# Transposes between the blocks of a sum, and a mixing norm whose first projections take unscaled rows

## What is computed

```
x = x + 0.5 * ffn(rms_norm(x, g_ffn1))
h = rms_norm(x, g_mix);  parts = split(h @ w_in)      # xr, gr, qb, ckv, qi, ki, wi, qc, kc, vc, f, ga, gb, gc
o_a = rglru(conv(xr)) * gelu(gr);  o_b = top-k latent attention(qb, ckv, qi, ki, wi);  o_c = forgetting attention(qc, kc, vc, f)
x = x + (sigmoid(ga)*(o_a@w0) + sigmoid(gb)*(o_b@w1) + sigmoid(gc)*(o_c@w2)) @ w_out
x = x + memory_cross_attention(rms_norm(x, g_xattn), rms_norm(mem, g_mem))
x = x + 0.5 * ffn(rms_norm(x, g_ffn2))
rms_norm(x, g) = x * rsqrt(mean(x*x) + 1e-6) * g;     ffn(h) = (silu(h@w_g) * (h@w_u)) @ w_down
```

## Time and profile before

| | |
|---|---|
| Median of 3 runs | 1418.57 us |
| The profiled execution: its time, its span | 1418.43 us, 1416.6 us |
| Mean granted TensorE clock | 0.997 |
| Busy: TensorE, VectorE, ScalarE, POOL | 1379.8, 945.6, 777.5, 132.3 us |
| HBM read | 241.18 MB |

### The profile page before, as it was taken

The page is one execution under the profiler, slowest core; times in us unless marked ns, Lnnn a source line. Parts: engine busy times, 40 slices in busy tenths (PEclk is TensorE's granted clock), DMA queues, the critical chain, the costliest instruction groups (busy, mean ns, idle before and its releaser), DMA issues.

```text
span 1416.6 us, 23830 instructions
## 1 busy us (share of the span) xinstructions
PE 1379.8 (97%) x8846; PEld 1228.3 (87%) x8846; DVE 945.6 (67%) x1456; ACT 777.5 (55%) x1378; POOL 132.3 (9%) x219
## 2 busy tenths in 40 slices
PE   6999999999999999999999999999999999999998
PEld 5888879988999888888888888898989989888886
DVE  5666666878666567666676666658777556666665
ACT  5554554745654466555564555566556445655544
POOL 4010000021420100000010000000224001100000
PEclk9999999999999999999999999999999999999999
DMA  8677664544545555666656667546454554466662
GB/s 239 187 205 208 196 179 149 163 138 148 170 132 175 183 144 165 191 180 199 184 174 185 198 185 205 149 136 201 134 160 138 166 191 144 129 203 179 198 187 74
DMA packets 286385, 243.38 MB, mean 172 GB/s; under 512 B 14345, under 2 KB 263609, under 8 KB 286305
## 3 DMA queue, kind: packets, MB, share of 16 engines
q1 hardware_dynamic: 284176, 236.77, 55.4%
q10 hardware_dynamic: 1600, 4.25, 0.9%
q0 software_dynamic: 528, 1.26, 0.5%
HBM read 241.18 MB, written 1.27 MB: 171 GB/s over the span
## 4 chain that ended last, share of the span: by engine, by line
issue 64%; PE 25%; DVE 3%; ACT 3%; POOL 2%; DVEq 1%; POOLq 1%; DMA 1%; ACTq 0%
PE work L1548 15%; PE work L1623 2%; PE work L1570 2%; PE acc L1585 1%; PE work L1627 1%; ACT w_hi L507 1%; POOL diag L721 1%; PE acc L1775 1%; DVE w_lo L515 1%; POOLq L720 1%; PE work L1763 1%; DVE score L1350 1%; ACT lg L1033 1%; DVEq L1238 0%; PE work L1698 0%
## 5 line engine op out<-in xcount | busy, mean ns | idle before, releaser
L515 DVE TENSOR_TENSOR w_lo<-raw,w_hi 128x1024 fp32r<-128x1024 f32 x444 | 550.5, 1260 | 105.8 <-ACT w_hi L507 104.2
L507 ACT ACTIVATE w_hi<-raw 128x1024 fp32r<-128x1024 f32 (+1 forms) x442 | 450.7, 1053 | 25.6 <-PE acc L1585 25.6
L1623 PE MATMUL work<-act,w_hi 128*128 128x512 f32 x1408 | 443.6, 396 | 9.5 <-DVE w_lo L515 5.5
L1548 PE MATMUL work<-act,w_hi 128*128 128x256 f32 x1696 | 317.8, 286 | 3.2 <-DVE act L1131 1.7
L1627 PEld LDWEIGHTS work<-act,w_lo 128*128 128x128 f32 x1408 | 265.0, 188 | 62.6
L1627 PE MATMUL work<-act,w_lo 128*128 128x256 f32 x1408 | 277.6, 279 | 0.0
L1548 PEld LDWEIGHTS work<-act,w_hi 128*128 128x128 f32 x1696 | 267.4, 191 | 10.4 <-issue 5.8
L1548 PE MATMUL work<-act,w_lo 128*128 128x256 f32 x848 | 239.8, 283 | 0.0
L1623 PEld LDWEIGHTS work<-act,w_hi 128*128 128x128 f32 x1408 | 217.8, 189 | 13.4 <-issue 10.4
L821 ACT ACTIVATE gu_s<-work 128x256 f32<-128x256 f32 x176 | 58.0, 382 | 202.7 <-PE work L1627 202.7
L1548 PEld LDWEIGHTS work<-act,w_lo 128*128 128x128 f32 x848 | 162.5, 192 | 0.6 <-issue 0.5
(11 more groups left out here) (238 smaller groups left out, 1722.5 us busy)
## 6 DMA issues: line engine op xcount, KB each, us to landing
raw<-in_ffn_w_gu SPq DMA_DIRECT2D x174, 512.0 KB, 5.0
raw<-in_w_in SPq DMA_DIRECT2D x52, 1024.0 KB, 5.2
raw<-in_ffn_w_down SPq DMA_DIRECT2D x44, 1024.0 KB, 4.9
raw<-in_w_branch SPq DMA_DIRECT2D x12, 1024.0 KB, 5.0
raw<-in_w_mkv SPq DMA_DIRECT2D x8, 1024.0 KB, 5.2
raw<-in_w_out SPq DMA_DIRECT2D x8, 1024.0 KB, 4.8
raw<-in_w_mq SPq DMA_DIRECT2D x4, 1024.0 KB, 5.3
raw<-in_w_mo SPq DMA_DIRECT2D x4, 1024.0 KB, 4.8
```

The costliest lines, as they stand in the source:

```text
L507: eng.activation(halves(w_hi, slot, kind, part), halves(raw, slot, kind, part), ACT.Copy)\
L515: eng.tensor_tensor(halves(w_lo, slot, kind, part), halves(raw, slot, kind, part), halves(w_hi, slot, kind, part).bitcast(F32), ALU.subtra ...
L1548: mm = pe.matmul(out_ps, ww[:, slot, first:first + width], xx[:, k, :], start=(k == 0 and n == 0), stop=(k == kn - 1 and n == 2))
L1623: pe.matmul(work[:, 2 * c + g, :], w_hi[:, slot, at_w:at_w + P], act[:, :, k, :], start=(k == 0), stop=False, skip_group_check=True)
```

## The change

1. Last unit of a sum: blocks in the order (0,0), (1,0), (0,1), (1,1); ahead of the last block TensorE makes the eight transposes of the next norm for k = 0 to 3 (`early_transposes`), the other eight follow after it (`late_transposes`; ahead of the memory attention, after `mk1`). All transposes go to the `acc` banks (`NT_BANK`).
2. Order on VectorE: residuals 0 to 2, three `norm_los`, residual 3, the rest (`residual_and_los`); one weight unit's `split_lo` that stood ahead of the residuals stands behind them. On ScalarE: norm_his 0 to 3, two squares, norm_his 4 to 7, two squares (`rows_of_x`).
3. Mixing norm: plain transposes of `x`, evacuated into `raw_hi` and `raw_lo`, from which `xr0` and `xr1` are projected; after `xr0` a new job `row` spreads `rstd` (`ones` by `diag`), ScalarE copies it to `rstd_row`. VectorE multiplies `xr` (`scaled_xr`) and, in PSUM, the transposed rows (`scaled_rows`, four of 128x512) by it; from these the scaled parts `act_hi` and `act_lo` are made a second time, for `gr0` and all behind.
4. `misc` in one pass of 208 columns; `ki` from it by two transposes, copied by ScalarE after its softplus chain.
5. Layer 1's first norm has its gains, its first two units' high parts and its early transposes inside the end of layer 0's `ffn2`. `last_hi`/`last_lo` and `nat` move to other places; the setup transposes go to `work` bank 3, so `vec_ready` is waited for ahead of `gate_up(1)`.

```diff
+BLOCKS = ((0, 0), (1, 0), (0, 1), (1, 1))
+NT_BANK = (0, 2, 1, 3)
+NT_SETS = (0, "raw", 1, 2, 3)
...
         self.norm(1)
         self.w_unit("xr0")
+        self.job("row")
         self.job("chan")
         for name in ("xr1", "gr0", "gr1"):
             self.w_unit(name)
         self.unit("misc")
-        self.job("ki")
         self.job("nat")
         self.job_of["misc"] = "nat"
         self.job(("rg", 0))
         self.job(("rg", 1))
         self.job("fT")
+        self.job("ki")
         self.job("ukT")
...
             if name[0] == "nt":
-                if name[1] == 1 or name[2] < 2:
-                    return acc2(name[2])
-                b = name[2] if name[1] in (0, 3) else PLAN.bank[("mq1", "mv0")[name[2] - 2]]
-                return work[:, b, :].rearrange("p (a b) -> p a b", a=2)
+                return acc2(NT_BANK[name[2]])
...
+            def rows_of_x(l, st, dst=act_hi):
+                norm_his(l, st, range(4), dst)
+                squares(l, st, (0, 1))
+                norm_his(l, st, range(4, KT), dst)
+                squares(l, st, (2, 3))
...
                 ffn(l, "ffn1")
-                squares(l, 1)
-                norm_his(l, 1)
+                rows_of_x(l, 1, raw_hi)
                 splits(a, split_hi, l, ("ffn1", RING * PAIRS - 1))
-
+                copy_out(l, "row", rstd_row[:], ps("row")[:, 0:SEQ])
+                for kk in range(KT):
+                    if kk % 2 == 0:
+                        a.wait_ge(nt_scaled, l * 4 + kk // 2 + 1)
+                    a.activation(act_hi[:, kk, :], ps2(("nt", 1, kk // 2))[:, kk % 2, :], ACT.Copy,
+                                 scale=gain[:, 1, kk:kk + 1]).then_inc(act_hi_ready, 1)
                 for j in range(2):
...
+            def residual_and_los(l, st, scale, n, order, hi=act_hi, lo=act_lo, late=True):
+                residual(l, st, scale, range(3))
+                norm_los(l, n, order, range(3), hi, lo)
+                residual(l, st, scale, (3,))
+                norm_los(l, n, order, range(3, KT if late else 4), hi, lo)
...
+                residual_and_los(l, 0, None, 1, 1, raw_hi, raw_lo)
+                splits(v, split_lo, l, ("ffn1", RING * PAIRS - 2))
                 splits(v, split_lo, l, ("ffn1", RING * PAIRS - 1))
+
+                def scaled_rows(j):
+                    nt = ps2(("nt", 1, j))
+                    v.tensor_tensor(nt, nt, rstd_row[:].unsqueeze(1).to_broadcast([P, 2, SEQ]), ALU.mult)\
+                     .then_inc(nt_scaled, 1)
+
+                def scaled_xr(j):
+                    wait_done(v, l, f"xr{j}")
+                    v.tensor_tensor(xr[:, 2 * j:2 * j + 2, CONV_W - 1:CONV_W - 1 + SEQ], ps2(f"xr{j}"),
+                                    rstd_row[:].unsqueeze(1).to_broadcast([P, 2, SEQ]), ALU.mult)\
+                     .then_inc(bank_of(f"xr{j}"), 1)
+
+                wait_evac(v, l, "row")
+                scaled_xr(0)
+                scaled_rows(0)
+                scaled_rows(1)
+                norm_los(l, 1, 2, range(2))
+                scaled_rows(2)
+                norm_los(l, 1, 2, range(2, 4))
+                scaled_rows(3)
+                norm_los(l, 1, 2, range(4, KT))
...
+                residual_and_los(l, 2, 1.0, 3, 5)
                 splits(v, split_lo, l, "mo0")
-                residual(l, 2, 1.0)
-                norm_los(l, 3, 4)
                 splits(v, split_lo, l, "mo1")
...
+                    all_gains(l + 1)
+                    residual(l, 3, None, range(3))
+                    norm_los(l + 1, 0, 0, range(3))
+                    residual(l, 3, None, (3,))
+                    norm_los(l + 1, 0, 0, range(3, KT))
+                    for part in range(2):
+                        split_lo(v, l + 1, (1, 0, 1), part)
...
+            def transposed(l, n, k, tt):
+
+                mm = pe.transpose(ps2(("nt", n, k // 2))[:, k % 2, tt * P:tt * P + P],
+                                  x[:, tt, k * P:(k + 1) * P], ident[:])
+                if tt == TT - 1 and k % 2:
+                    mm.then_inc(job_done, 1)
+
+            def early_transposes(l, n):
+
+                pe.wait_ge(x_ready, l * 16 + 4 * n + 2)
+                for k in range(KT // 2):
+                    for tt in range(TT):
+                        transposed(l, n, k, tt)
+
+            def late_transposes(l, n):
+
+                pe.wait_ge(x_ready, l * 16 + 4 * n + 3)
+                for k in (4, 5):
+                    transposed(l, n, k, 0)
+                pe.wait_ge(x_ready, l * 16 + 4 * n + 4)
+                for k in (4, 5):
+                    transposed(l, n, k, 1)
+                for k in (6, 7):
+                    for tt in range(TT):
+                        transposed(l, n, k, tt)
 
             def rstd_rows(l, st):
...
-                    for tt in range(TT):
-                        for nh in range(2):
-                            for kk in range(2):
-                                mm = group(kk, tt, nh)
-                            mm.then_inc(acc_done, 1)
+                    for b, (tt, nh) in enumerate(BLOCKS):
+                        if b == 3 and norm:
+                            early_transposes(*norm)
+                        for kk in range(2):
+                            mm = group(kk, tt, nh)
+                        mm.then_inc(acc_done, 1)
...
-                two_tiles(l, "xr0", wait_k=1)
+                two_tiles(l, "xr0", x_hi=raw_hi, x_lo=raw_lo, wait_k="raw")
+                wait_free(pe, l, "row")
+                pe.wait_ge(rstd_ready, l * 12 + 4)
+                for tt in range(TT):
+                    mm = pe.matmul(ps("row")[:, tt * P:tt * P + P], ones[:], diag[:, tt, :], start=True, stop=True)
+                mm.then_inc(job_done, 1)
                 wait_free(pe, l, "chan")
                 pe.wait_ge(params_landed, l * 192 + 192)
                 pe.matmul(ps("chan")[:, 0:8 * BT], chan_in[:], ident[0:8 * BT, 0:8 * BT], start=True, stop=True)\
                   .then_inc(job_done, 1)
-                for name in ("xr1", "gr0", "gr1"):
-                    two_tiles(l, name)
+                two_tiles(l, "xr1", x_hi=raw_hi, x_lo=raw_lo)
+                two_tiles(l, "gr0", wait_k=1)
+                two_tiles(l, "gr1")
                 u = unit("misc")
-                wait_free(pe, l, "ki")
-                columns(l, u, "ki", 0, P, ps("ki")[:, 0:SEQ], act_hi, act_lo, KT).then_inc(job_done, 1)
                 wait_free(pe, l, "nat")
-                rows(l, u, lambda tt: ps("nat")[:, tt * NAT:tt * NAT + NAT], (HD, MISC), act_hi, act_lo)\
+                rows(l, u, lambda tt: ps("nat")[:, tt * MISC:tt * MISC + MISC], (0, MISC), act_hi, act_lo)\
                     .then_inc(job_done, 1)
                 pe.wait_ge(xc_ready, l + 1)
                 rg_gates(0)
                 rg_gates(1)
                 wait_jobs(pe, l, ["nat"], "fT")
                 for tt in range(TT):
-                    mm = pe.transpose(ps("fT")[0:HEADS, tt * P:tt * P + P], nat[:, tt, NAT - HEADS:NAT], ident[:])
+                    mm = pe.transpose(ps("fT")[0:HEADS, tt * P:tt * P + P], nat[:, tt, F_AT:MISC], ident[:])
+                mm.then_inc(job_done, 1)
+                wait_free(pe, l, "ki")
+                for tt in range(TT):
+                    mm = pe.transpose(ps("ki")[0:HD, tt * P:tt * P + P], nat[:, tt, 0:HD], ident[:])
...
-                for name in ("mq1", "mv0"):
-                    wait_free(pe, l, name)
-                part_transposes(l, 2, 0, range(KT))
-                part_transposes(l, 2, 1, range(KT // 2))
+                             lambda kk, j=j: pe.wait_ge(mrg_ready, l * 4 + j + 1), (l, 2))
+
                 filler(l, "mk1")
-                part_transposes(l, 2, 1, range(KT // 2, KT))
+                late_transposes(l, 2)
                 two_tiles(l, "mq0", wait_k=2)
                 two_tiles(l, "mq1")
```

More of the change, by code:

```diff
@@ L299, in block_kernel @@
         ki = at("ki", [P, SEQ])
-        nat = at("nat", [P, TT, NAT])
+        nat = at("nat", [P, TT, MISC], over="qc")
         c_nat = at("c_nat", [P, TT, LAT])
@@ L877, in ffn @@
                 nxt(at + 1, 1)
+                if l == 0 and st == "ffn1":
+                    a.wait_ge(t5_landed, 16 * (P // ROWS))
                 h_high(FT - 2, dst=last_hi)
@@ L908, in left @@
                         a.wait_ge(bank_free[3], l * PLAN.uses[3] + 1)
+                    elif c == 1 and l:
+                        wait_sum(a, l - 1, ("ffn2", RING * PAIRS - 2), 1)
                     else:
@@ L1108, in _ @@
                 splits(a, split_hi, l, "mo0")
-                squares(l, 3, range(3))
-                norm_his(l, 3, range(4))
-                squares(l, 3, (3,))
-                norm_his(l, 3, range(4, KT))
+                rows_of_x(l, 3)
                 splits(a, split_hi, l, "mo1")
@@ L1220, in ffn @@
                     splits(v, split_lo, l, (st, at + 2))
-                    splits(v, split_lo, l, (st, at + 3))
             def filler(l, name):
```

(43 more changed lines are left out.)

121 lines of the change are left out of this document (53 added, 68 removed).

## The result

The median of 12 executions after the change is 1421.14 us (1419.7 to 1425.85). The kernel before, run beside it, had 1418.57 us (12 executions). The ratio is 1.0021, its 95% interval 1.0013 to 1.0029: slower, where 1414.4 and faster were forecast. The profiled execution took 1422.01 us, its span is 1420.2 us and its mean granted clock 0.993 (before 0.997).

The account below looks back on a forecast made before the run. TensorE bounds the kernel, busy 1379.8 of 1416.6 us (97%). Terms 1.3 + 7.5 + 0.7 - 5.1 - 0.25 = 4.1 us off the profiled 1418.43 give 1414.3; the runs' median is 0.14 above: 1414.4 us, range 1404 to 1419.

Parts of the forecast that it names:

- The start: Kernel start: `act` waits for four transposes instead of ten; 1.3 us gained, 0 if the weights' DMA is the later.
- The first tile of `ffn2`: Entry into a feed-forward stage: first matmul at t = 8.4 instead of 8.85, 0.45 us gained.
- a hole: Before `rstd_rows` at feed-forward entries: TensorE ready at 14.0, `rstd` at 16.1, so 2.1 us of new idle time.
- the three entries: Into `ffn2` twice and `ffn1` of layer 1: hole 2.1, gain 0.45, so 1.7 us lost each, 5.1 together.
- From the last sum unit to the wait for `lg`: Mixing stages: `qi0` at t = 44.3 instead of 49.0 and 47.1; 4.7 and 2.8 us gained, 7.5 together.
- The memory attention: Entry into memory attention, twice: the `act` wait of 0.35 us before `mq0` goes; 0.7 gained, at least 0.
- the end: Kernel end: a later square may make POOL's first chain meet VectorE's final multiply; 0 to 0.5 us lost, 0.25 taken.
- rival (3): New holes of 2 us bring low-clock stretches at 1.35 us each; three of them give 1418.5. Chance 0.12.
- (1): POOL's `rstd` chain is not held up by `split_lo`: 14.2 us gained, 1404.3. Chance 0.22.
- (2): Each POOL step waits for two `split_lo` halves: `rstd` at 17.2 in five places, 5.4 us more, 1419.8. Chance 0.12.
- (4): VectorE becomes the bound between `row` and `nat`: multiplies at 1.3 instead of 0.7 us give 1421.6. Chance 0.09.
- The rule on `split_lo` and POOL: A VectorE instruction with two SBUF inputs keeps a GpSimd instruction reading SBUF waiting until it ends; chain 5.0 us, alone 2.3.

Follow-up runs that it names:

- e1: The kernel after with 1152 unused bytes behind `ki`, so `h_hi`, `h_lo` and all behind stand at their old addresses: 1417.71 us.
- e4: The kernel before with `nat` over `qc`, so `h_hi`, `h_lo` and all behind stand 1152 bytes lower: 1422.86 us, ratio to before 1.0027.
- e9: e1 plus a wait: at three feed-forward entries VectorE begins its four `split_lo` halves only once `rstd` of both token tiles is made: 1409.3 us.
- e3: The kernel after with squares of blocks (0,0) and (1,0) ahead of norm_his 0 to 3, the others ahead of 4 to 7: 1412.17 us.
- e12: e3 with addresses moved: `h_hi`, `h_lo` at remainder 128 by 256, `act` at 192: 1399.4 us, ratio to before 0.9865.

## Why the prediction was wrong

**The terms for the edits were right.** With the old addresses, in an execution without low clock behind the new holes (e1), they come out nearly as worked out. The start gains 1.3. The first tile of `ffn2` comes 0.5 us earlier (0.45 forecast), the row product after it 2.0 us later relative to that tile (a hole of 1.9, 2.1 forecast), and the three entries lose 4.9 us (5.1 forecast). From the last sum unit to the wait for `lg` 4.5 and 3.1 us are gained (forecast 4.7 and 2.8, from `qi0`). The memory attention gains 0.2 in each layer (0.35 forecast), the end loses 0.4 (0.25). These sum to 4.1 us, as forecast. That the whole span gives 4.1 as well is luck: 1.5 gained by the missing low stretch at 295 and 1.4 lost in the varying part of the layers nearly cancel.

**The step that failed: a term put at nothing, the move of `nat`.** The prediction worked out the work and the waits of each edit, and gave the moves of `last_hi` and `nat` no sentence of their own, which priced them at nothing. The move shifts what lies behind `nat` by 1152 bytes, and 960 matmuls step 3.8 ns slower: 3.6 us, shown both ways round (e1, e4). Nothing in the traces of before pointed at it by itself; the mean step of the sums was 229.6 ns where other matmuls of 512 columns had 233, which could have been asked about.

**The step that failed by its size: rival (3), the clock.** Its mechanism was right and named. The chance of 0.12 came from "the old idle of 3.16 brought one in one layer only". One of two cases is no argument for a tenth, and the trace of before had two more, the waits of 1.68 us for `lg`, one of them with a low stretch (295.4); the runs have 8 of 15 at 1.9 us. The price was 1.35 and measured 1.6; 3.4 us at half the clock can cost 1.7, and here work fills all of it. Counted by stretches it is 2.6 us that the sum should have carried: 1414.4 + 2.6 + 3.6 = 1420.6, beside 1421.14 measured. But filling the holes gave back only 1.5 us by the medians, 2.7 by the ratios. So 0.4 to 1.6 us is left open.

**The rivals.** (1), POOL not held up, was not what happened; with POOL free at the three entries (e9) the time is 8.4 us under e1's, 7.1 by the ratios to before. (2) fell: the steps took about one half's time each, 0.85 to 1.34 us, though e3 has one of 2.64 us. (4) fell: the multiplies by the row took 0.65 to 0.69 us, also from PSUM into PSUM; its upper bound of 1.3 was too high by its own row, since 512 columns at twice the time that `split_lo` takes for each are 1.2, which is under the 1.27 at which it would have decided. The rule on `split_lo` and POOL that was weighed (the Trainium skill, SBUF — State Buffer, Who interferes with whom) holds in these traces in the main: 4.9 us against 2.3 with the splits put off; the step of 2.64 us in e3 was held for longer than one such instruction, which is more than the rule says.

**The range.** The missing term alone gives 1418.0, the clock alone 1417.0, both within 0.2% of before; together they pass 1419, where the range ended: the prediction took such cases for alternatives, not for terms that add.

## What to carry to other kernels

List every tile whose address a change shifts, and compare the step of the matmuls (distance of starts, over a stretch without waits) before and after; 64 bytes were worth 2.4 us here by the steps, and from e3 to e12, which differ in addresses alone, the ratio to before went from 0.9945 to 0.9865. Price a new hole in TensorE's row above its own length, by how often a low stretch follows a hole of that length, the old ones included, and look at several executions, since a single profile showed three of three in one kernel and none of three in its twin. And where POOL makes something small that TensorE waits for, keep VectorE's operations on two SBUF inputs out of its way, by order or by a wait.

## What was not expected of the hardware

- The step of a matmul depends on where its operands start, by remainder of the address by 256 bytes. Sums of 512 columns, `h` loaded as weights, the moving operand at 128: 233.4 ns at 192, 232.4 at 0, 229.6 at 64, 227.1 at 128. At 64 the three products differ (medians 232, 226 and 229 ns in e1), at 192 and 128 they are alike. With `act` as the moving operand: 232.9 at 128, 229.7 at 192. Why is open.
- Behind idle time of 1.9 us the granted clock fell to 1.2 GHz for 3.4 us in 8 of 15 cases, 0.1 to 1.4 us after TensorE was at work again; at 1.7 us in 18 of 34, at 1.3 us in 3 of 24; at holes of 3.4 us in three of three, twice for 6.8 us; and not in the same places filled with transposes.
